# Output projection of the attention layers from seven quadrant products instead of eight

## What is computed

```python
# first (even) layer: attention with top-k selection (o_a) beside gated linear attention (o_b)
o_a = o_a.reshape(B, S, A_W) * jax.nn.silu(ga)
...
o_b = o_b.reshape(B, S, B_VW) * jax.nn.silu(gb)
x = x + jnp.concatenate([o_a, o_b], axis=-1) @ w_out_even[i]     # 512x1024 @ 1024x1024
# second (odd) layer begins
h = rmsnorm(x, norm_odd[j])
proj = h @ w_in_odd[j]
```

## Time and profile before

| what | value |
|---|---|
| median of 3 runs | 522.53 us (522.23 to 522.89) |
| profiled execution | 522.31 us |
| its span, first to last instruction | 520.3 us |
| instructions in the span | 7739 |
| granted TensorE clock, mean | 0.996 of full speed |

### The profile page before, as it was taken

The page is one execution under the profiler, slowest core; times in us unless marked ns, Lnnn a source line. Parts: engine busy times, 40 slices in busy tenths (PEclk is TensorE's granted clock), DMA queues, the critical chain, the costliest instruction groups (busy, mean ns, idle before and its releaser), DMA issues.

```text
span 520.3 us, 7739 instructions
## 1 busy us (share of the span) xinstructions
PE 505.1 (97%) x2855; PEld 408.1 (78%) x2855; DVE 355.3 (68%) x742; ACT 244.6 (47%) x407; POOL 297.0 (57%) x184
## 2 busy tenths in 40 slices
PE   7999999999999999999999999998899999999994
PEld 7876888788888888888888889886677767788883
DVE  3795599769957456556471055899788898759824
ACT  6734744233221344644461355287656665257413
POOL 5380755736734076556415315589999999860701
PEclk9999999999999999999999999999999999999998
DMA  8443354222222002200263402516655562412004
GB/s 269 123 146 122 122 183 142 83 83 82 82 81 83 1 0 83 83 0 1 78 248 88 135 20 65 151 34 172 159 152 163 162 163 82 130 74 81 1 0 161
DMA packets 47762, 53.14 MB, mean 102 GB/s; under 512 B 5480, under 2 KB 33155, under 8 KB 47726
## 3 DMA queue, kind: packets, MB, share of 16 engines
q1 hardware_dynamic: 47726, 52.66, 33.4%
HBM read 44.03 MB, written 2.12 MB: 89 GB/s over the span
## 4 chain that ended last, share of the span: by engine, by line
PE 83%; DVE 8%; ACT 2%; issue 2%; SPq 2%; POOL 1%; DMA 0%; POOLq 0%; ACTq 0%
PE bank L1585 30%; PE bank L1605 29%; PE bank L1803 3%; PE bank L1730 3%; DVE r_va L1131 2%; PE bank L1780 2%; PE bank L1894 2%; DVE top L1129 2%; PE bank L1881 2%; PE bank L1792 2%; SPq L467 2%; DVE r_ob L1115 1%; PE bank L1621 1%; PE bank L1520 1%; PE bank L1669 1%
## 5 line engine op out<-in xcount | busy, mean ns | idle before, releaser
L573 POOL TENSOR_TENSOR w_lo<-w_raw,w_hi 128x2048 fp32r<-128x2048 f32 (+1 forms) x31 | 140.1, 4524 | 98.6 <-ACT w_hi L731 97.6
L1585 PE MATMUL bank<-hT_lo,w_hi 128*128 128x512 f32 (+1 forms) x280 | 111.1, 397 | 0.0
L1585 PE MATMUL bank<-hT_hi,w_hi 128*128 128x512 f32 (+1 forms) x280 | 110.3, 394 | 0.0
L1585 PE MATMUL bank<-hT_hi,w_lo 128*128 128x512 f32 (+1 forms) x280 | 109.6, 391 | 0.0
L1605 PE MATMUL bank<-w_hi,hT_hi 128*128 128x512 f32 x252 | 101.9, 404 | 0.0
L1605 PE MATMUL bank<-w_hi,hT_lo 128*128 128x512 f32 x252 | 98.4, 391 | 0.0
L1605 PE MATMUL bank<-w_lo,hT_hi 128*128 128x512 f32 x252 | 98.3, 390 | 0.0
L731 ACT ACTIVATE w_hi<-w_raw 128x2048 fp32r<-128x2048 f32 (+1 forms) x35 | 65.7, 1880 | 40.6 <-PE bank L1605 35.3
L1385 DVE SCALAR_TENSOR_TENSOR bank<-r_va,pvec,bank 128x512 f32<-128x512 f32 x94 | 68.0, 752 | 4.7 <-PE bank L1894 3.2
L653 POOL TENSOR_TENSOR r_g<-r_g 128x512 f32<-128x512 f32 x48 | 62.3, 1298 | 10.3 <-ACT r_g L924 4.5
L1585 PEld LDWEIGHTS bank<-hT_lo,w_hi 128*128 128x128 f32 (+1 forms) x280 | 52.3, 187 | 16.4 <-issue 5.9
(11 more groups left out here) (237 smaller groups left out, 768.3 us busy)
## 6 DMA issues: line engine op xcount, KB each, us to landing
w_raw<-in_w_in_even_dram SPq DMA_DIRECT2D x14, 1024.0 KB, 5.3
w_raw<-in_w_in_odd_dram SPq DMA_DIRECT2D x16, 512.0 KB, 5.0
w_raw<-in_w_out_even_dram SPq DMA_DIRECT2D x4, 1024.0 KB, 8.3
w_raw<-in_w_in_odd_dram SPq DMA_DIRECT2D x4, 1024.0 KB, 6.1
w_raw<-in_w_out_odd_dram SPq DMA_DIRECT2D x4, 1024.0 KB, 5.2
r_att<-r_va SPq DMA_DIRECT2D x32, 64.5 KB, 2.5
r_ka<-r_qkb SPq DMA_DIRECT2D x32, 64.5 KB, 2.4
r_x<-in_x_dram SPq DMA_DIRECT2D x4, 512.0 KB, 5.9
```

The lines of the kernel that those rows point to most:

```text
L573: nc.gpsimd.tensor_tensor(v(w_lo[j % 3]), v(w_raw[j % 2]), v(w_hi[j % 3]).bitcast(F32), ALU.subtract).then_inc(lo_ready, 1)
L1585: ins = nc.tensor.matmul(proj_bank(g)[0:m, :], w[:, k, P * i:P * i + m], h[:, k, :], start=(n == 0), stop=(n == 3 * KC - 1))
```

## The change

The mixed rows are cut in early rows (0 to 255) and late rows (256 to 511), and in a (columns 0 to 511, from the attention heads) and b (512 to 1023). The 1024x1024 matrix is cut in four quadrants. Seven products of a row quadrant (or a sum of such) by a weight quadrant (or a sum) replace the eight: `MIX = ("late b", "late a", "s1", "s2", "s3", "early a", "s4")`. Each has one slot (16 to 22) and two units of twelve matmuls, which makes 168. From product 4 on, four of them go on top of what already stands in a bank. The slots of the odd layer are now numbered from 23 and those after it from 35.

Weights: slots 16 and 17 are loaded as before (only their order by quadrant differs). The other two quadrants are loaded into r_att (b12) and r_ka (b22). GpSimd makes t1 and t3, VectorE t2 and t4, each a difference of 128x2048, and slots 18 to 22 are split from them. Rows: VectorE makes s1 to s4 and their low parts, ScalarE their high parts. VectorE adds 14 banks to x (`mix_add`) instead of 8. GpSimd splits 3 slots more than before and its four `rsqrt` stand after `split_lo(23)`.

```diff
+MIX = ("late b", "late a", "s1", "s2", "s3", "early a", "s4")
...
-    s += b("oe", 0, B_FIRST) + b("oe", 512, B_FIRST)
+    s += [("s", up[4:8], [(0, "oe", 0, 512)]), ("s", up[0:4], [(0, "oe", 0, 512)])] + [("t", (), [])] * (len(MIX) - 2)
...
+                if j == S_OE:
+                    sp.wait_ge(ob_summed, TB)
+                    sp.dma_start(r_att[:, 0:2048].rearrange("p (k n) -> p k n", k=4), WSRC["oe"].rearrange(
+                        "(k p) n -> p k n", p=P)[:, 4:KC, 512:1024]).then_inc(b12_in, 16)
                 if j == S_OE + 2:
+                    sp.wait_ge(qk_done, NSTEP)
+                    sp.dma_start(r_ka[:, 0:2048].rearrange("p (k n) -> p k n", k=4), WSRC["oe"].rearrange(
+                        "(k p) n -> p k n", p=P)[:, 0:4, 512:1024]).then_inc(b22_in, 16)
...
-                if s_ == S_OE + 3:
+                if s_ == S_OE:
+                    pool.wait_ge(b12_in, 16)
+                    pool.wait_ge(lo_ready, S_OE + 1)
+                    nc.gpsimd.tensor_tensor(w_raw[0][:], r_att[:, 0:2048], w_raw[0][:], ALU.subtract).then_inc(t1_ready, 1)
+                    pool.wait_ge(t1_ready, 1)
+                    pool.wait_ge(b22_in, 16)
+                    nc.gpsimd.tensor_tensor(r_att[:, 0:2048], r_att[:, 0:2048], r_ka[:, 0:2048],
+                                            ALU.subtract).then_inc(t3_ready, 1)
+                if s_ == S_ODD - 1:
                     for t in range(TB):
                         rsqrt(t, t + 1, var_ready, TB + t + 1, rstd_ready)
...
+            split_hi(S_OE + 3)
+            act.wait_ge(s2_ready, 2)
+            nc.scalar.activation(s2_hi, s2, ACT.Copy).then_inc(mix_hi, 1)
+            split_hi(S_OE + 4)
+            act.wait_ge(s3_ready, 2)
+            nc.scalar.activation(s3_hi, s3, ACT.Copy).then_inc(mix_hi, 1)
+            split_hi(S_OE + 5)
+            act.wait_ge(s4_ready, 2)
+            nc.scalar.activation(s4_hi, s4, ACT.Copy).then_inc(mix_hi, 1)
+            mix_square(2, 0, 0, 3)
+            mix_square(3, 0, 1, 4)
+            split_hi(S_OE + 6)
+            mix_square(0, 1, 2, 9)
+            mix_square(1, 1, 3, 10)
+            split_hi(S_ODD)
+            mix_square(0, 0, 4, 11)
+            mix_square(1, 0, 5, 12)
+            split_hi(S_ODD + 1)
+            mix_square(2, 1, 6, 13)
...
+            def low_in_place(s, s_lo, s_hi, hi):
+                dve.wait_ge(mix_hi, hi)
+                nc.vector.tensor_tensor(s_lo, s, s_hi.bitcast(F32), ALU.subtract).then_inc(mix_low, 1)
+            def mix_add(b, t, half, unit):
+                dve.wait_ge(mix_unit, unit)
+                xs = x_t[:, t, 512 * half:512 * half + 512]
+                nc.vector.tensor_tensor(xs, bank[b][:], xs, ALU.add).then_inc(mix_added, 1)
...
+            nc.vector.tensor_tensor(s1, s2, late_b, ALU.add).then_inc(s1_ready, 1)
+            nc.vector.tensor_tensor(r_qa[:], r_ka[:, 0:2048], w_raw[0][:], ALU.subtract).then_inc(t2_ready, 1)
+            nc.vector.tensor_tensor(hT_lo[:, 4:KC, EARLY], four_chunks(s1), hT_hi[:, 4:KC, EARLY].bitcast(F32),
+                                    ALU.subtract).then_inc(mix_low, 1)
...
+            low_in_place(s2, s2_lo, s2_hi, 8)
+            mix_add(6, 2, 0, 1)
+            mix_add(7, 3, 0, 2)
+            dve.wait_ge(t2_ready, 1)
+            dve.wait_ge(lo_ready, S_OE + 2)
+            nc.vector.tensor_tensor(w_raw[1][:], w_raw[1][:], r_qa[:], ALU.subtract).then_inc(t4_ready, 1)
+            dve.wait_ge(mix_added, 2)
+            mix_add(4, 2, 0, 3)
+            mix_add(5, 3, 0, 4)
+            low_in_place(s3, s3_lo, s3_hi, 9)
+            mix_add(2, 0, 1, 5)
+            mix_add(3, 1, 1, 6)
+            mix_add(6, 2, 1, 7)
+            low_in_place(s4, s4_lo, s4_hi, 10)
+            mix_add(7, 3, 1, 8)
+            mix_add(6, 0, 1, 9)
+            mix_add(7, 1, 1, 10)
...
+            mix_add(6, 0, 0, 11)
+            mix_variance(0)
+            mix_add(7, 1, 0, 12)
             scale_rows(0, TB + 1)
+            mix_variance(1)
             scale_rows(1, TB + 2)
+            mix_add(2, 2, 1, 13)
+            mix_variance(2)
...
+            MIX_BANK = {"late b": 6, "late a": 4, "s1": 2, "s2": 6, "s3": 6, "early a": 6, "s4": 2}
+            SPLIT = {"late b": 2, "late a": 6, "s1": 7, "s2": 8, "s3": 9, "early a": 4, "s4": 10}
+            FREED = {"s2": 1, "s3": 7, "early a": 9, "s4": 5}
+            def mixed_unit(n, t):
...
+                elif name in FREED:
+                    pe.wait_ge(mix_added, FREED[name] + t)
...
+                pe.wait_ge(mix_hi, SPLIT[name])
+                for q in range(3):
+                    if q == 2:
+                        pe.wait_ge(mix_low, SPLIT[name])
+                    for i in range(4):
+                        hi, lo = mix_operand(n, i, t)
+                        ins = nc.tensor.matmul(b[:], lo if q == 2 else hi, (wl if q == 1 else wh)[:, i, :],
+                                               start=(n < 3 and q == 0 and i == 0), stop=(q == 2 and i == 3),
+                                               skip_group_check=True)
+                ins.then_inc(mix_unit, 1)
```

More of the change, by code:

```diff
@@ L400, in wait_slot_used, with raw @@
                 eng.wait_ge(group_done, FIRST[j] + (1 if j == 1 else 2))
-            elif j % 2:
+            elif S_OE <= j < S_ODD:
+                eng.wait_ge(mix_unit, 2 * (j - S_OE) + 2)
+            elif j in BEGINS:
+                eng.wait_ge(half_used, BEGINS.index(j) + 1)
+            else:
                 eng.wait_ge(group_done, FIRST[j] + TB)
-            else:
-                eng.wait_ge(half_used, sum(1 for i in range(0, j + 1, 2) if SLOTS[i][0] == "b"))
+        def raw(j):
+            if S_OE + 2 <= j < S_ODD:
+                return {S_OE + 2: w_raw[0], S_OE + 3: r_qa, S_OE + 4: r_att, S_OE + 5: w_raw[1], S_OE + 6: r_ka}[j][:, 0:2048]
+            return w_raw[j % 2][:]
         def proj_bank(g):
@@ L730, in split_hi @@
                     v = lambda t: t[:]
[L731 to L737, removed]
+                nc.scalar.activation(v(w_hi[j % 3]), v(raw(j)), ACT.Copy).then_inc(hi_ready, 1)
             def half_high(base, half, half_bank, scale, chunks=range(KC)):
@@ new lines, in _ @@
+            for n in range(2):
+                act.wait_ge(mixed_T, 5 + n)
+                nc.scalar.activation(hT_hi[:, 2 * n:2 * n + 2, 0:HALF], two_chunks(4 + n), ACT.Copy).then_inc(mix_hi, 1)
+            split_hi(S_OE + 2)
+            for n in range(2):
+                act.wait_ge(mixed_T, 7 + n)
+                nc.scalar.activation(hT_hi[:, 2 * n:2 * n + 2, HALF:S], two_chunks(n), ACT.Copy).then_inc(mix_hi, 1)
+            act.wait_ge(s1_ready, 1)
+            nc.scalar.activation(hT_hi[:, 4:KC, 0:HALF], four_chunks(s1), ACT.Copy).then_inc(mix_hi, 1)
@@ L1505, in _ @@
             pe.wait_ge(pool_chain, 2)
-            def transpose_blocks(order, blocks, ready, bank_of):
-                for n, t in blocks:
-                    ready(n, t)
-                    ins = nc.tensor.transpose(bank[bank_of(n)][:, P * t:P * t + P], hx(t, order[n]), ident[:])
-                    if t == TB - 1:
-                        ins.then_inc(hT_in_bank, 1)
-            LOW, HIGH = range(4), range(4, KC)
-            ROWS_1 = [(n, t) for part in (LOW, HIGH) for t in range(TB) for n in part]
             def keep_clock(n, dst):
@@ L1594, in unit_b @@
                 ks = SLOTS[j][1]
-                first, final = j % 2 == 0, j % 2 == 1
+                first, final = j in BEGINS, j not in BEGINS
                 if first and part[0] == 0:
@@ L1858, in odd_rows @@
                             ins.then_inc(hT_in_bank, 1)
-            for s_ in range(S_OE, S_ODD):
-                slot_ready(s_)
-                for t in range(TB):
-                    if s_ == S_ODD - 1 and t == TB - 1:
+            for n in range(len(MIX)):
+                slot_ready(S_OE + n)
+                for t in range(2):
+                    if n == 0 and t == 1:
+                        pe.wait_ge(mix_low, 2)
+                        pe.wait_ge(late_kept, 2)
+                        pe.wait_ge(mixed_a, 2)
+                        quad_transposes(0, 2, 0)
+                        pe.wait_ge(oa_emptied, TB)
+                    if n == len(MIX) - 1 and t == 1:
                         odd_rows(0)
-                    unit_b(s_, t, hT_base=R_MIX if s_ < S_OE + 2 and t == 0 else None)
+                    mixed_unit(n, t)
             def group_half(i, half, between={}):
```

225 lines of the change are left out of this document (168 added, 57 removed).

## The result

| | kernel before | changed kernel |
|---|---|---|
| median | 522.71 us (522.23 to 522.91, 4 runs) | 528.43 us (528.16 to 528.45, 4 runs) |
| ratio, 95% interval | | 1.011 (1.0092 to 1.0127) |
| profiled execution, its span | 522.31, 520.3 | 528.45, 526.6 |

The prediction was 529.6 us, +7.1. Measured are +5.7 in the medians and +6.3 in the spans, slower by more than the 0.2% that can be told. The path it took is the one of the main case, with two terms of its sum too large and with a part of the clock rival in it.

What follows compares the result with a forecast made beforehand. TensorE, busy 97% of the span, was taken as the bound. Stops of 12.25 us less 5.45 for removed matmuls gave +6.8, with 0.3 for restarts +7.1: 529.6 us, range 524.5 to 533.5.

Steps and rivals of the forecast that it cites:

- main case: Output projection: VectorE operations with two SBUF inputs wait for GpSimd's splits, TensorE stops; 527 to 532 us, chance 0.68.
- clock rival: Before unit 9: 4.9 us of TensorE idle halves the clock, +0.9 to +3.6, 530.5 to 533.2 us; chance 0.14.
- What is removed: TensorE in the output projection: 192 matmuls become 168, 5.45 us less, all on the chain.
- Start: Head of the output projection: t3 holds L1292, third eight transposes wait 0.3 us, unit 1 starts at 265.9.
- Unit 7: Product s2: its low part is held by `split_lo(19)` to 283.4, ends at 284.6; TensorE stops 2.0 us.
- Unit 9: Product s3: t4, held by `split_lo(20)`, ends at 291.4; additions behind it end at 295.5; TensorE stops 4.9 us.
- Unit 10: Low part of s4 meets `split_lo(21)`, ends at 299.4, addition 8 at 300.0; TensorE stops 1.8 us.
- Odd rows: Before the next norm's transposes: load, then square roots behind `split_lo(23)`; stops of 1.7 and 0.8 us.
- First group: Slot 23: `half_high(0)` starts 1.1 us behind the transposes instead of 0.26; another 0.75 us.
- nine operations of the held form: VectorE: late b (two), s1, low parts of s1 to s4, t2, t4, held while GpSimd splits; 0.69 to 2.3 us unheld.
- no holding: Rival: the nine VectorE operations keep their lengths; -0.8, 521.7 us, or 519.7 with a fast load; chance 0.14.
- whole gain: Rival: no holding, and the square roots find GpSimd free too; -5.4, 517.1 us; chance 0.04.

Runs made afterwards that it cites:

- run 1: Changed kernel with GpSimd's six splits of slots 18 to 23 left out, memsets of the same total length in their place: 521.37 us, 0.9994 of the kernel before.
- run 8: Changed kernel with splits of slots 19, 21, 23 and t3 on VectorE, t2 on GpSimd, VectorE's and ScalarE's orders made to suit: 518.43 us, 0.992 of the kernel before.
- run 5: The changed kernel again, unedited, on another chip: 528.85 us, 1.0116 of the kernel before.
- run 2: Changed kernel with the square roots of blocks 0 and 1 ahead of `split_lo(23)` on GpSimd: 530.13 us, 1.0169 of the kernel before.
- run 3: Changed kernel with memsets for the splits of slots 18 to 23 and the first two square roots ahead of the last: 520.79 us, 0.9971 of the kernel before.
- run 4: Changed kernel with 17 and 40 small useless matmuls ahead of units 7 and 9 to keep the clock up: 529.81 us, 1.0152 of the kernel before.
- run 7: Changed kernel with `split_lo(23)` moved from GpSimd to VectorE, right behind addition 13: 526.48 us, 1.0071 of the kernel before.

## Why the prediction was right, and where it was not

- **What is removed:** as said. The chain lost its 24 matmuls, and runs 1 and 8 show them as time once nothing holds.
- **Start:** L1387 (L1292 before) took 2.86 us from 262.07 instead of 1.75 and so ended at 264.9 (said: 265.0), unit 1 started at 265.84 (265.9).
- **Unit 7:** the low part of s2 ended at 284.8 (284.6), the stop was 2.04 (2.0). Right.
- **Unit 9:** t4 ended at 291.4 and unit 9 started at 295.66 (291.4 and 295.6), but the stop was 2.81 instead of 4.9 since unit 8 ended at 292.85 instead of 290.7.
- **Unit 10:** the low part of s4 ended at 299.3 (299.4) and addition 8 at 299.9 (300.0), but there was no stop. What took the place of these 2.1 and 1.8 us is TensorE's own time, most of it the lower clock. The stretch from 285.48 to 292.85 holds two units, 5.44 us by my price, and took 7.37; at full clock the same two took 5.83 in run 5 (285.75 to 291.58). The stretch from 295.66 to 311.30 holds five, 13.6 by my price, and took 15.64; at full clock the same five took 14.02 in run 1 (288.80 to 302.82). So the two stretches are 4.0 us longer than I had them, about the 3.9 that the two stops lost: 3.2 by the clock and 0.8 by a unit price of 2.72 that is too low there.
- **Luck in it:** unit 11 started at 302.88, as the walk has it, because the slowed unit 9 ended just behind addition 8. In run 5 it ended later, and unit 11 started at 303.91.
- **Clock:** I had made it a rival at 0.14 with the trigger at 4.9 us of idle time. The mechanism was right, the trigger too high: it fell after 2.04. The trace before had this: asked in finer steps, it shows the clock falling at 516.0, 2.3 us behind the end of the last matmul (513.7); the edge of the earlier trace rows at 516.00 hid it. In one execution the fall cost nothing, in another (run 5) 0.8 us. That lies within the main range, but as separate cases the two were badly cut: both happen in the same kernel.
- **Odd rows, the term that was mis-sized:** I took 6.8 us for the pair of loads, from the earlier trace rows. In the changed kernel they were issued at 298.21, and `split_hi(23)` started at 304.44, right behind a square, with no wait for a DMA: at most 6.2 us. This is the low bound that I had named, -0.6. The first stop was 0.96 (said: 1.7), the second 0.52 (0.8).
- **First group:** `half_high(0)` started 0.75 us behind the start of unit 14 (315.47) instead of 1.1, so TensorE's stop grew from 0.20 to 0.37. From the last unit to the first 512-column matmul behind the group (L1760, L1585 before) it took 17.31 us (314.72 to 332.03) against 16.88 before (309.12 to 326.00): +0.43 instead of +0.75.
- **Sum:** the last unit started at 314.72, 5.6 later than the earlier trace rows (said: 6.0), the matmul behind the group 6.0 later, and the span is 6.3 longer. The 0.8 us between +7.1 and +6.3 are, within rounding, the 0.4 up to the last unit and the 0.3 of the first group.
- **Not foreseen:** `split_lo(23)` also held L1507, a 128x1 operation, for 3.6 us. Addition 12 behind it came 2.6 late. It cost nothing only because the square root waited for the same split (it started at 311.12, right behind the split's end at 311.03). I had counted nine operations of the held form and overlooked this tenth, since I had looked for wide ones only.
- **Rivals:** no holding is excluded by run 1, in which its condition is made true and its time appears. The "whole gain" at 517.1 had as its condition the square roots ahead of the split; run 2 shows that this doesn't suffice (3.45 us of stop behind the held scaling), and run 3 that the scaling is held even by a GpSimd operation that only writes.

What stays open: the 1.4 us between the measured and the expected time of run 4 don't lie in the output projection, whose units start where they did in the changed kernel. In its trace the first L1760 matmul comes at 331.95 (changed kernel: 332.03) and the last stretch of 168 matmuls at 480.42 (479.17). So 1.3 us lie between, in the odd layer, which no edit touches and which took 146.2 to 148.6 us between these two points in the twelve traces. Why it varies no run settles. Nor was it tried whether the scaling on ScalarE would free it from GpSimd.

## What to carry to other kernels

Before work is moved to "idle" engines, count for VectorE and GpSimd together the time of the operations that exclude each other, and lay it beside the stage; two engines at half load can be full as a pair. Give such work to the engine that does it in the shorter time, even if it is the busier one (2.28 against 4.6 us here), and let the slower one run beside operations with an input in a bank. An order of one engine and the size of the pieces only shift the held time, which gave 2.7 us here with one order (526.2) and nothing with smaller pieces (529.7); taking time out of the pair, with an order made to suit, removes it (518.4).

## What the runs showed of the hardware

- Even the smallest operation with two inputs in SBUF was held: 128x1 (L1507) took 3.61 us beside a split, 0.16 without.
- One with a single input, the scaling from SBUF to SBUF, was held by a split (4.73 instead of 0.48 us) and by a memset (2.00 and 2.10), while operations with two inputs kept 1.23 and 2.28 us beside memsets. Not every one with a single input is held: two of 128x1 (L1500) took 0.33 us together beside the split from 306.42, as in run 1 with GpSimd idle.
- When both wait, VectorE goes first between two operations of GpSimd: a split lasts 5.63 instead of 4.62 us behind one held operation, and four quarters 8.14 us instead of 5.0 where two operations, the low part of s2 and t4, went in between.
- The granted clock fell to 1.2 GHz after 2.04 us without a matmul in one execution and stayed at 2.4 GHz after 2.01 us in another of the same kernel. In the trace before it fell 2.3 us behind the last matmul. Behind stops of 2.04 and 1.97 us in runs 2 and 7 it fell only when four matmuls had run at full clock.
